# Modulation products moved behind three norms, three projections in rounded passes, chunk-by-chunk units and one subtraction on another engine, in a two-block model kernel

## What is computed

```python
for i in range(2):                       # D = 1024, 512 tokens in layer 0
    mod = silu(c) @ ada_w[i] + ada_b[i]  # ada_w[i]: 1024 x 6144, for c and for c_ctx
    sh1, s1, g1, sh2, s2, g2 = split(mod, 6)
    h = rms_norm(x) * (1 + s1) + sh1     # gains left out here
    x = x + g1 * mixer(h)                # ends with a 1024 x 1024 projection
    h = rms_norm(x) * (1 + s2) + sh2
    x = x + g2 * conv_ffn(h)             # 1024 -> 2 x 2816, conv over 3 tokens, silu * value, -> 1024
x = rms_norm(x)
```

## Time and profile before

| | |
|---|---|
| the runs | 2400.62 us (2398.37 to 2402.69) |
| the profiled execution | 2402.18 us, span 2400.4 us |
| mean granted TensorE clock | 0.918 |
| PE busy | 83% (1983.6 us) |
| VectorE, ScalarE, POOL busy | 37%, 28%, 4% |
| DMA | 592.24 MB, mean 247 GB/s |
| chain that ended last | PE 55%, DMA 28%, VectorE 4%, ScalarE 3% |

### The profile page before, as it was taken

The page is one execution under the profiler, slowest core; times in us unless marked ns, Lnnn a source line. Parts: engine busy times, 40 slices in busy tenths (PEclk is TensorE's granted clock), DMA queues, the critical chain, the costliest instruction groups (busy, mean ns, idle before and its releaser), DMA issues.

```text
span 2400.4 us, 37512 instructions
## 1 busy us (share of the span) xinstructions
PE 1983.6 (83%) x16396; PEld 1470.4 (61%) x16396; DVE 899.1 (37%) x1580; ACT 663.2 (28%) x1200; POOL 99.8 (4%) x113
## 2 busy tenths in 40 slices
PE   5998899999998999999999998666666656666665
PEld 4996655888786896899897466433333333334332
DVE  3445624434523327465575354322211211111112
ACT  4333414223423326445453302111111111111111
POOL 0010101000002002000100000000000000000000
PEclk9998999999999999999999998888888888888888
DMA  6306842222223221453540247999999999999996
GB/s 269 141 36 268 356 184 79 96 105 76 71 87 145 106 107 61 148 193 127 194 175 10 90 206 287 427 426 427 426 427 427 427 417 426 427 427 427 427 427 285
DMA packets 45698, 592.24 MB, mean 247 GB/s; under 512 B 5677, under 2 KB 5865, under 8 KB 9568
## 3 DMA queue, kind: packets, MB, share of 16 engines
q1 hardware_dynamic: 42112, 580.21, 59.1%
q0 software_dynamic: 2992, 8.57, 1.1%
q10 hardware_dynamic: 432, 1.06, 0.1%
HBM read 588.77 MB, written 1.05 MB: 246 GB/s over the span
## 4 chain that ended last, share of the span: by engine, by line
PE 55%; DMA 28%; DVE 4%; ACT 3%; issue 2%; DVEq 0%; ACTq 0%
DMA s_ring<-in_w_up 12%; PE bank L626 10%; PE bank L628 10%; PE bank L627 10%; PE bank L1295 6%; DMA s_arena<-in_w_up 5%; DMA s_xT<-in_w_up 5%; DMA s_hT<-in_w_up 3%; PE bank L1319 2%; PE bank L687 1%; PE bank L889 1%; PE bank L676 1%; PE bank L1236 1%; PE bank L1325 1%; DMA s_ring<-in_slabs 1%
## 5 line engine op out<-in xcount | busy, mean ns | idle before, releaser
L626 PE MATMUL bank<-s_arena_r 128*128 128x256 f32 (+2 forms) x1656 | 542.4, 328 | 35.1 <-DVE s_hT_r L2045 23.1
L1447 ACT ACTIVATE s_arena<-bank 32x256 f32<-32x256 f32 (+8 forms) x415 | 166.8, 409 | 1035.4 <-PE bank L1295 558.7
L628 PE MATMUL bank<-s_arena_r,s_ring_r 128*128 128x512 f32 (+2 forms) x1312 | 441.6, 337 | 0.0
L1295 PE MATMUL bank<-s_ring,s_arena 128*32 128x256 f32 x2048 | 299.0, 512 | 130.9 <-DMA s_xT<-in_w_up 40.7
L627 PE MATMUL bank<-s_hT_r,s_arena_r 128*128 128x512 f32 (+2 forms) x1096 | 367.9, 336 | 0.0
L626 PEld LDWEIGHTS bank<-s_arena_r 128*128 128x128 f32 x1656 | 313.3, 189 | 71.0 <-issue 27.2
L2040 DVE TENSOR_TENSOR s_ring_r<-s_ring,s_arena_r 128x2048 fp32r<-128x2048 f32 (+1 forms) x93 | 225.8, 2429 | 263.9 <-ACT s_arena_r L1447 263.7
L1295 PEld LDWEIGHTS bank<-s_ring,s_arena 128*32 128x32 f32 x2048 | 144.8, 146 | 208.6 <-issue 196.8
L628 PEld LDWEIGHTS bank<-s_arena_r,s_ring_r 128*128 128x128 f32 x1312 | 250.0, 191 | 27.2
L2654 DVE TENSOR_TENSOR s_arena<-s_arena,bank 64x256 f32<-64x256 f32 x64 | 27.1, 423 | 528.2 <-ACT s_arena L1447 528.2
L1447 ACT ACTIVATE s_arena_r<-s_ring 128x2048 fp32r<-128x2048 f32 (+1 forms) x93 | 187.5, 2019 | 127.6 <-PE bank L628 127.6
(11 more groups left out here) (356 smaller groups left out, 2648.6 us busy)
## 6 DMA issues: line engine op xcount, KB each, us to landing
s_ring<-in_slabs SPq DMA_DIRECT2D x72, 2048.0 KB, 8.5
s_ring<-in_w_up SPq DMA_DIRECT2D x33, 2048.0 KB, 33.9
s_ring<-in_w_down SPq DMA_DIRECT2D x31, 2048.0 KB, 28.7
s_ring<-in_w_gate SPq DMA_DIRECT2D x31, 2048.0 KB, 33.2
s_arena<-in_w_gate SPq DMA_DIRECT2D x16, 2048.0 KB, 33.0
s_arena<-in_w_up SPq DMA_DIRECT2D x16, 2048.0 KB, 32.3
s_arena<-in_w_down SPq DMA_DIRECT2D x15, 2048.0 KB, 28.9
s_ring<-in_slabs SPq DMA_DIRECT2D x16, 1408.0 KB, 6.4
```

The costliest lines, as they stand in the source:

```text
L626: mm(out, w_hi_, x_hi_, start=start, stop=False)
L628: return mm(out, w_lo_, x_hi_, start=False, stop=stop)
L1295: last = mm(pb[b][32 * q:32 * q + 32, 0:256], x[:, c, :], w[q // 2][:, c, 256 * (q % 2):256 * (q % 2) + 256], start=c == 0, stop=c == DC - ...
L1447: return act.activation(out, in_, func, **kw)
```

## The change

- `ADA_BATCH` has eleven batches, of which eight with 13 groups lie in the scan; groups 17, 18 and 19 are computed behind the last unit of the first projection, 20 and 21 behind the first feed-forward, 22 and 23 behind the second projection, each time into bank 6 and ahead of PE's wait for the norm (`gap_rows`). Their reading and transposing come later (`gap_read`, `gap_turn`, `gap_columns`). The slabs of 17, 18, 22 and 23 go to free parts of the arena (slots 4 to 7), those of 19, 20 and 21 to ring slots; the conditioning vectors (`ada_sc`) move from the arena to `ones`.
- The first projection has units 0 and 1 plain and 2 to 7 split, with four units ahead of the last y instead of five; the second projection likewise; the last projection is wholly split, in 16 half units. Their weights and inputs are rounded by ScalarE and subtracted by VectorE.
- The first two units of each feed-forward take the chunks together, and so do the first four query units of layer 1.
- The rest of the second half of that first slab is taken by VectorE, ahead of the factors of the second norm, and not by POOL.
- The meta tokens' load and square move into the second feed-forward. The rounding of the feed-forwards' first weights moves between the squares, their subtraction between the residual additions.

```diff
-ADA_BATCH = [2, 3, 3, 3, 3, 2, 2, 2]
+ADA_BATCH = [2, 2, 2, 2, 2, 1, 1, 1, 3, 2, 2]
+ADA_SCAN = 8
...
-    for g in range(ADA_EARLY, 2 * ADA_N):
+    for g in range(ADA_EARLY, ADA_AT[ADA_SCAN]):
...
             add("ffn_w_in", l, j, DC, 512, ("ffn_in_mm", 44 * l + 4 * j + 4), slot())
+            if j == 0 and l == 0:
+                late(17, 4, ("o_mm", HEADS))
+                late(18, 5, ("o_mm", HEADS))
+                late(19, slot(), ("gla_y_tr", HEADS))
+            if j == 0 and l == 1:
+                late(22, 6, ("na_o_mm", NA_H))
+                late(23, 7, ("na_o_mm", NA_H))
         for m in range(DC):
             add("ffn_w_out", l, m, FC, P, ("ffn_out_mm", 8 * l + m + 1), slot())
+            if l == 0 and m >= DC - 2:
+                late(20 + m - (DC - 2), slot())
...
+            def gap_rows(b):
+                if b > ADA_SCAN:
+                    pe.wait_ge(S["ada_late"], b)
+                for i in range(ADA_BATCH[b]):
+                    ada_products(ADA_AT[b] + i, pb[6], P * i)
...
             def ffn(l, T, norm):
                 for i in range(FC):
+                    if i == 3:
+                        gap_turn(ADA_SCAN + 2 * l)
+                    if i == 0:
+                        first = [halves_of(place_r[in_slab(l, 0)], j) for j in range(2)]
+                        pe.wait_ge(S["w_lo"], W_GLA + (W_FFN + W_NA) * l + 2)
+                        for c in range(DC):
+                            pe.wait_ge(S["h_lo"], H_AT[2 * l + 1] + c + 1)
+                            for j in range(2):
+                                for a in range(2):
+                                    last = split_mm(pb[2 * j + a][:, 0:T], w_hi[j][:, c, a, :], first[j][:, c, a, :], h_hi[:, c, 0:T], hT_r[:, c, 0:T],
...
+            def gla_out(m, ks):
+                w, o, bank = FIRST["gla_out"] + m // 4, 128 * (m % 4), pb[m % GLA_AHEAD][:, :]
+                if m < PLAIN:
+                    got(w)
+                    for k in ks:
+                        last = mm(bank, place[w][:, k, o:o + 128], g_qk[:, 4 * (k % 2) + k // 2, :], start=k == 0, stop=k == DC - 1, skip_group_check=True)
+                    return last
+                pe.wait_ge(S["w_lo"], W_GLA_OUT + m - PLAIN + 1)
...
+            gap_rows(ADA_SCAN)
             pe.wait_ge(S["proj_x"], 2 * DC)
             pe.wait_ge(S["rstd_ready"], norms["n2_0"][1] + 1)
             ffn(0, TT, "n1_1")
+            gap_rows(ADA_SCAN + 1)
             pe.wait_ge(S["rstd_ready"], norms["n1_1"][1] + 1)
...
-                        for u in range(2):
+                        for u in range(4):
...
+                if part == 0:
+                    gap_turn(ADA_SCAN + 1)
+            pe.wait_ge(S["ada_late"], ADA_SCAN + 2)
...
-            project("na_out", lambda k: n_o[:, k, :], NT, 2 * DC, 1, "n2_1")
+            na_project()
+            gap_rows(ADA_SCAN + 2)
...
+            def channels(ct, part):
+                o, q = NT * (ct % 2), DC * part + ct
+                pe.wait_ge(S["w_lo"], W_OUT2 + q + 1)
+                for i in range(HC):
+                    k = HC + i if part == 0 else i
+                    if ct == 0:
+                        pe.wait_ge(S["h_lo"], H_OUT2 + HC * part + i + 1)
+                    last = split_mm(pb[ct // 2][:, o:o + NT], c_hi[q % 8][:, i, :], w2_of(place_r, q)[:, i, :], y_hi(k), y_lo[:, k, N_META:T2],
...
-            pool.wait_ge(S["late_decayed"], A_NA_W + 1)
-            pool.tensor_tensor(half(place_r[w1], 1), half(place[w1], 1), w_half[1].bitcast(F32), ALU.subtract).then_inc(S["late_decayed"], 1)
             pool.wait_ge(S["ffn_out_mm"], DC)
-            pool.dma_start(meta, d["metaT"].rearrange("(c p) t -> p c t", p=P)).then_inc(S["meta_in"], 16)
...
             ffn(0, TT)
+            w1 = FIRST["na"]
+            dve.wait_ge(S["late_decayed"], A_NA_W + 1)
+            TTn(half(place_r[w1], 1), half(place[w1], 1), w_half[1].bitcast(F32), ALU.subtract).then_inc(S["late_decayed"], 1)
             dve.wait_ge(S["ffn_out_x"], 2 * DC)
             norm_split("n1_1", 2, TT)
...
                 for i in range(FC):
+                    if l and i == 12:
+                        act.wait_ge(S["meta_in"], 16)
+                        A(meta_sq, meta, ACT.Square).then_inc(S["mix_act"], 1)
```

325 lines of the change are left out of this document (234 added, 91 removed).

## The result

The changed kernel took 2370.27 us (median of four runs, 2367.41 to 2376.53) against 2400.69; the ratio is 0.9879, with a 95% interval of 0.9863 to 0.9894. The profiled execution took 2367.41 us (span 2365.6), 34.8 less than the profiled one before, while the medians differ by 30.4. Where these four come from is part of what follows.

What follows compares the result with a forecast made beforehand. PE time before the experts' weight stream starts was taken as the bound; terms from scan to last projection sum to -34.5, taking the profiled 2402.2 to 2367.7, median 2366 us; forecast range 2357 to 2376, with rivals 2355 to 2384.

Steps and rivals of the forecast that it cites:

- The scan, -13: First mixer's scan: seven modulation groups fewer ahead of VectorE's waits for scores save 13 us, bounds -17 and -5.
- the sum of 15.3: Scan: savings at heads 1, 3, 5, 6 and 7 together, before some 2.3 us taken off for half clock.
- Rival 1: The scan gives only 5 us, as VectorE's chain or half clock replaces the waits; 2374, up to 2384 us; chance 0.15.
- rival 3: Scan: without the moved groups PE's clock falls and the kernel gets slower, 2444 us if wholly at half clock; chance 0.05.
- First projection, -7.9: First projection: six split units of eight products, each 0.164 us cheaper, save 7.9 us, with nothing late.
- the second rival: Split products run at the skill page's column rate: 5.2 us more gained in three places, 2361 us; chance 0.05.
- First norm, -1.8: Behind the first norm: three groups fill PE's idle time and keep it warm, units go chunk by chunk; 1.8 us less.
- Second norm, -4.6: Second norm: VectorE instead of POOL subtracts, chunks come 2.0 us earlier, four units go together; 4.6 us less.
- Second projection and third norm, -3.9 and +1.8: Split products save 3.9 us in the second projection; later copy and subtraction ahead of the factors cost the norm 1.8.
- Last projection, -5.1: Last projection: all 64 products split at 0.0805 us each save 5.1 us and start the experts' stream earlier; bounds -3 and -6.
- the 22 that the prediction named as a sign: Sign of being right: the first feed-forward's first rounded matmul comes some 22 us earlier.
- rival 4: The experts' stream doesn't start earlier by the last projection's gain: 2371 us; chance 0.05.

Runs made afterwards that it cites:

- The second try at the feed-forward's weights: The changed kernel with the second feed-forward's first weights rounded ahead of those of projection units 5 and 7, and subtracted in that order; 2370.31 us, ratio 0.9873.
- the short scan: The changed kernel with each of the 13 groups in the scan computing only the last of its eight chunks; 2371.56 us, ratio 0.9884.

## Why the prediction came out right

**The scan, -13.** The mechanism holds: the waits for scores fell from 20.15 to 7.1 us, and putting the groups back restores them. The size was 12.05 in the two first profiles; over all profiles 137.8 before and 127.9 after, 9.9. Two parts of the sum of 15.3 were mis-sized. One is head 5: the group gave 2.3 us there in the forecast, but the wait for scores had covered one for ScalarE, which now shows with 1.76 us (2.15 in the whole scan). The other is the 2.3 us taken off for the clock.

The second try at the feed-forward's weights drew a clock of 0.91 in its scan, as high as the 0.90 of the first profile before, and its scan took 125.80 us: 13.0 less than 138.84, and all of it is accounted for by the waits for scores (20.15 to 6.88), the group of the last turn (some 1.8) and the 2.15 us for ScalarE against them. The 3.1 us from there to the mean of 9.9 go with the clock: among the profiles of the changed kernel and its variants the scan takes 128.9 us at 0.85, 127.4 at 0.87, 126.8 at 0.88 and 125.8 at 0.91. So the -13 is right for an equal clock, where the forecast had meant it with the clock's cost in it, and that is luck in part. Rival 1 (the scan gives only 5, because something else takes the place of the waits, the half clock for one) had the direction of both, at a greater size; rival 3 (the clock turns the move into a loss) names the second, and the short scan shows that it takes all of the gain when nearly all of the remaining products go.

**First projection, -7.9:** 7.7, and 7.6 when undone. The trace's price of a product held. By the column rate of the Trainium skill, "TensorE: Matmul & The Clock Gate" (Wait — 56ns, not 53.3ns?), which was the second rival, the three projections would have given 5.2 us more. The trace disagrees: the changed kernel's split products go at 864 in 200 us at 512 columns (390 to 590 us), which is the 0.232 of the earlier trace rows once more.

**First norm, -1.8:** 1.0, by the means 0.8. Both halves of the argument were right as to what happens (full clock, 28 matmuls in 6 us). What was missed is PE's idle time of 0.51 to 1.15 us ahead of the third group's last four records, in eight profiles; less this time the stage is 377.9 us in each of them, 1.4 below the mean before. Where it is absent (first projection plain) the stage took 377.56, 1.7 below, nearly the forecast. Its cause stays open. With it, the groups end 1.2 to 1.9 us after the first chunk is there, and that is what the clock gave back: without the groups the stage is as long (378.54).

**Second norm, -4.6:** 5.4. Of these 2.1 are POOL's subtraction (2.0 forecast) and 2.9 the four units. Some 0.7 lies in the attention between the last split product and the projection (53.84 us against 54.52). Of it 0.6 is one wait of PE for VectorE at 905.91 us, 0.59 us long, which the changed kernel doesn't have; with all groups in the scan it is 1.44 us and the attention 55.36. Why VectorE is late there stays open.

**Second projection and third norm, -3.9 and +1.8.** The first term failed: 2.3. The products did save 3.6 (the last one ends 24.3 us behind the start instead of 27.9), but with units of 2.8 us the preparation of the feed-forward's weights no longer fits between two residual additions, and 1.3 of it came back through VectorE, POOL and the sum of squares. I had costed the move of that preparation only behind the last square, where its 2.45 us were about right (2.3 against before, with plain products).

**Last projection, -5.1:** from its first product to the load 51.7 before and 46.7 after, 5.0.

**The total.** The sum of -34.5 met the profile's -34.8, and that was partly luck: the means add to -30.7, the medians differ by 30.4. The forecast of the median passed from one profile to a median by a constant of 1.6 us, when the two profiles drew different clocks in the scan and in the second block. The first rounded matmul of the first feed-forward came 18.0 us earlier (391.98 to 373.96) and not the 22 that the prediction named as a sign; its own terms give 20, and by them the waits for scores should have ended at 6.6 us, not at the 5 it names (7.1 measured). No run showed the start of the stream held by anything else (rival 4), and none was slower than before (rival 3).

## What to carry to other kernels

Cost a moved piece of work by what waits behind it at its old place, and then by how long the gaps are at its new one: the same preparation that fitted between units of 5.6 us broke the chain at 2.8. Taking work out of a stage of alternating engines pays only as far as the clock doesn't fall with it; here the last 22 us of products taken out gave nothing. A wait that goes may uncover another behind it, as at head 5. And when single profiles of one kernel differ by more than the effect sought, compare stages at full clock, look within them for idle time that comes and goes, and take the others as means or at an equal clock.

## What was not expected of the hardware

- Of two profiles of the same kernel, one was 8.3 us longer in span, 7.2 of it in stages with a lower mean granted clock (0.91 or 0.83 for 1.00 in 20 us windows of the second block), while stages at full clock repeated to 0.1 us, but for the first norm's. These dips came at different places from run to run, and what one costs depends on whether a wait stands behind it.
- PE sat idle 0.51 to 1.15 us ahead of the last four records of a modulation group behind the first norm, in eight profiles, with nothing in the profile that it waited for.
- Taking 22.2 us of matmul work out of a 129 us stage left its length unchanged; the clock fell from 0.85 to 0.74.
- GpSimd's addition of 128x256 took 0.74 us alone and 2.27 to 2.64 us beside VectorE's subtraction from two SBUF tiles, ending 0.6 us behind it each time, and VectorE's factor 2.81 us beside GpSimd's subtraction: the blocking goes both ways.
